# First layer of a fused two-block transformer kernel: decay's logarithm later, its square and the memory keys' scaling on ScalarE, recurrent parts in the MLP's buffer

## The reference, cut to what matters

```python
proj = h @ w_in;  u, gate, xq = split(proj, [512, 1024])
u = conv4(u) + conv_b                                  # depthwise, width 4
r = sigmoid(block_diag(u, w_r) + b_r); i = sigmoid(block_diag(u, w_i) + b_i)
log_a = -8.0 * r * softplus(-lam)                      # softplus needs a log1p
a = exp(log_a)
b = sqrt(-expm1(2.0 * log_a)) * (i * u)
hs = scan(h_t = a_t * h_{t-1} + b_t);  y = hs * gelu(gate)
k, v = split(rms_norm(mem) @ w_kv, 2)                  # memory keys and values
q, k = rms_norm(xq per head), rms_norm(k per head)     # 4 heads of 128
y_mem = softmax(q k^T / sqrt(128)) v
x = x + concat(y, y_mem) @ w_out
```

## Time and profile before

| | |
|---|---|
| median of 3 runs | 1368.66 us (1366.49 to 1369.4) |
| the profiled execution's own time | 1368.92 us |
| its span in the profile | 1366.8 us |
| TensorE busy | 1326.5 us, 97% of the span |
| VectorE busy | 869.9 us, 64% |
| ScalarE busy | 716.1 us, 52% |
| the chain that ended last | PE 83%, DVE 9%, ACT 3%, POOL 2% |
| mean granted TensorE clock | 0.988 of full speed |
| mean ScalarE copy of a unit, line 983 | 1048 ns |
| mean VectorE split of a unit, line 1538 | 1212 ns |

### The profile page before, as it was taken

How to read it: one execution, slowest core, us unless ns; L and a number is a source line. 1 busy time by engine, 2 the same in 40 slices (tenths; PEclk the granted TensorE clock), 3 DMA queues, 4 the chain that set the end, 5 groups by cost and what they waited for, 6 DMA issues and landing times.

```text
span 1366.8 us, 18745 instructions
## 1 busy us (share of the span) xinstructions
PE 1326.5 (97%) x7309; PEld 1132.7 (83%) x7309; DVE 869.9 (64%) x1154; ACT 716.1 (52%) x1177; POOL 122.1 (9%) x158
## 2 busy tenths in 40 slices
PE   6879999999999999999999999999999999999998
PEld 5868888887888888888988778888889887788887
DVE  4775656657645666567775666666676755666665
ACT  5565544546565545446554455555565444555553
POOL 2101100004201200003101020000021000100000
PEclk9999999999999999999999999999999998999999
DMA  9433655455423555545632145555356211555551
GB/s 363 165 123 122 232 186 197 172 186 201 170 80 121 200 199 186 186 172 192 206 111 76 48 170 186 193 187 196 136 199 218 93 63 62 172 190 189 189 186 46
DMA packets 62327, 224.43 MB, mean 164 GB/s; under 512 B 7192, under 2 KB 7328, under 8 KB 62240
## 3 DMA queue, kind: packets, MB, share of 16 engines
q1 hardware_dynamic: 59616, 214.23, 45.3%
q0 software_dynamic: 1904, 6.82, 1.5%
q10 hardware_dynamic: 720, 2.19, 0.4%
HBM read 222.16 MB, written 1.05 MB: 163 GB/s over the span
## 4 chain that ended last, share of the span: by engine, by line
PE 83%; DVE 9%; ACT 3%; POOL 2%; issue 2%; DMA 0%; ACTq 0%; POOLq 0%; DVEq 0%
PE ps L277 16%; PE ps L323 15%; PE ps L282 15%; PE ps L281 15%; PE ps L327 8%; PE ps L433 3%; PE ps L468 2%; DVE wlo L1538 2%; PE ps L330 2%; PE ps L491 2%; PE ps L797 2%; PE ps L329 1%; DVE xn L1577 1%; ACT xn L1020 1%; PE ps L472 1%
## 5 line engine op out<-in xcount | busy, mean ns | idle before, releaser
L1538 DVE TENSOR_TENSOR wlo<-raw,whi 128x1024 fp32r<-128x1024 f32 (+1 forms) x402 | 479.5, 1212 | 270.2 <-ACT whi L983 268.4
L983 ACT ACTIVATE whi<-raw 128x1024 fp32r<-128x1024 f32 (+1 forms) x409 | 424.1, 1048 | 289.7 <-PE ps L323 178.9
L323 PE MATMUL ps<-XT,whi 128*128 128x512 f32 x896 | 318.6, 399 | 0.0
L327 PE MATMUL ps<-XT,wlo 128*128 128x256 f32 x896 | 251.5, 281 | 0.0
L323 PEld LDWEIGHTS ps<-XT,whi 128*128 128x128 f32 x896 | 168.4, 188 | 41.1
L277 PE MATMUL ps<-whi,HT_hi 128*128 128x512 f32 (+1 forms) x496 | 187.5, 378 | 1.5 <-DVE wlo L1538 1.0
L282 PE MATMUL ps<-whi,HT_lo 128*128 128x512 f32 (+1 forms) x496 | 186.3, 376 | 0.0
L281 PE MATMUL ps<-wlo,HT_hi 128*128 128x512 f32 (+1 forms) x496 | 186.2, 375 | 0.0
L327 PEld LDWEIGHTS ps<-XT,wlo 128*128 128x128 f32 x896 | 169.3, 189 | 1.2
L277 PE MATMUL ps<-whi,XT 128*128 128x512 f32 (+1 forms) x304 | 122.5, 403 | 6.9 <-DVE wlo L1538 4.6
L282 PE MATMUL ps<-whi,XT 128*128 128x512 f32 (+1 forms) x304 | 118.0, 388 | 0.0
(11 more groups left out here) (254 smaller groups left out, 1845.1 us busy)
## 6 DMA issues: line engine op xcount, KB each, us to landing
raw<-in_w_m SPq DMA_DIRECT2D x152, 512.0 KB, 4.2
raw<-in_w_n SPq DMA_DIRECT2D x108, 512.0 KB, 4.2
raw<-in_w_c SPq DMA_DIRECT2D x48, 512.0 KB, 3.8
raw<-in_w_o SPq DMA_DIRECT2D x32, 512.0 KB, 3.5
raw<-in_w_kv SPq DMA_DIRECT2D x16, 512.0 KB, 4.5
raw<-in_w_b SPq DMA_DIRECT2D x16, 512.0 KB, 4.2
raw<-in_w_w SPq DMA_DIRECT2D x16, 512.0 KB, 5.5
raw<-in_w_a SPq DMA_DIRECT2D x12, 512.0 KB, 8.8
```

Source lines behind the costliest of these rows:

```text
L323: m = pe.matmul(outs[f][:, :], hi[:, j, at], both, start=(k == 0), stop=False)
L327: pe.matmul(outs[f][:, 0:T], lo[:, j, at], XT[0][:, k, :], start=False, stop=False)
L983: act.activation(whi[:, g % NSPLIT, 0:w], raw[:, g % NRAW, 0:w], ACT.Copy).then_inc(split_hi, 1)
L1538: dve.tensor_tensor(wlo[:, g % NSPLIT, 0:w], raw[:, g % NRAW, 0:w], whi[:, g % NSPLIT, 0:w].bitcast(F32), ALU.subtract).then_inc(split_lo, 1)
```

## The change

Five edits, all in layer 0:

1. On VectorE the `log1p` of the decay and the four small steps behind it stand after the convolution and not before the queries' sums. ScalarE waits for the biases (`hb`) ahead of the gates, and for the decay's constants (`lru_c`) only ahead of the decay.
2. (decay + 1)^2 is one Square on ScalarE; VectorE's two products become one.
3. The keys' scaling moves from two VectorE instructions of 128x512 to eight of 128x128 on ScalarE. Around it, one more unit's copy stands ahead of the square root, and VectorE splits unit 19 ahead of gelu.
4. The high and low parts of y go into `HT_hi` and `HT_lo`, `out_first` reads them there, and ScalarE's wait for the last product of `mv0` is gone.
5. In this attention's softmax VectorE makes the splits of units 20 to 22 one a step (`slowly`), where they stood together ahead of y's low part.

```diff
-            def out_first(L, w):
+            def out_first(L, w, rows=MX):
-                        linear(names, banks, [a[w][4 * nb + u]], 2, tok(MX), 2 * u, KT, opened=(u == 0))
+                        linear(names, banks, [a[w][4 * nb + u]], 2, tok(rows), 2 * u, KT, opened=(u == 0))
-            out_left = out_first(0, "w_o0")
+            out_left = out_first(0, "w_o0", tuple(h[:, 0] for h in HT))
...
-            act.wait_ge(ev("lru_c"), 1)
+            act.wait_ge(ev("hb"), 1)
             for g, dst in ((0, 1), (1, 2)):
...
             act.wait_ge(bank_free[fills["rg0.1"].bank], fills["rg0.1"].turn)
+            act.wait_ge(ev("lru_c"), 1)
             for dst, fn, c in ((11, ACT.Tanh, "lh"), (7, ACT.Exp, "lc")):
                 for f in range(4):
                     at = slice(f * T, (f + 1) * T)
-                    m = act.activation(slot(dst, 1024)[:, at], slot(1, 1024)[:, at], fn, bias=sm(c, 4)[:, f:f + 1],
-                                       scale=sm(c, 4)[:, f:f + 1])
-            m.then_inc(ev("decay"), 1)
+                    act.activation(slot(dst, 1024)[:, at], slot(1, 1024)[:, at], fn, bias=sm(c, 4)[:, f:f + 1],
+                                   scale=sm(c, 4)[:, f:f + 1]).then_inc(ev("decay"), 1)
+            act.wait_ge(ev("decay"), 8)
+            act.activation(slot(4, 1024), slot(7, 1024), ACT.Square, bias=1.0).then_inc(ev("decay2"), 1)
...
-            splits(fills["mk0.0"].pos)
+            splits(fills["mk0.0"].pos + 1)
             act.wait_ge(ev("b2"), 1)
...
             rows_in("mk0", hrow[:, :, :].rearrange("p a b -> p (a b)"), None)
+
+            act.wait_ge(ev("frstd"), 2)
+            for tt in range(TT):
+                ps = full(f"mk0.{tt}")
+                for h in range(4):
+                    m = act.activation(slot(5, 1024)[:, tt * BLK + h * P:tt * BLK + (h + 1) * P], ps[:, h * P:(h + 1) * P], ACT.Copy,
+                                       scale=sm("rk8", 8)[:, 4 * tt + h:4 * tt + h + 1])
+                free(f"mk0.{tt}", m)
...
             mem_keys_in(0)
-            splits(fills["mv0.1"].pos + AHEAD)
-            f = fills["mv0.1"]
-            act.wait_ge(bank_full[f.bank], f.turn)
             act.wait_ge(ev("yrow"), 1)
-            act.activation(MX[0][:, 0:4, :].rearrange("p f t -> p (f t)"), slot(4, 1024), ACT.Copy).then_inc(ev("yhi"), 1)
+            act.activation(HT[0][:, 0, :, :].rearrange("p f t -> p (f t)"), slot(4, 1024), ACT.Copy).then_inc(ev("yhi"), 1)
...
-            def soft(tags, between):
+            def soft(tags, between, slowly=False):
...
-                    ps = full(f"{tag}.s{i}", 0 if n else NSPLIT)
+                    ps = full(f"{tag}.s{i}", 0 if n or slowly else NSPLIT)
...
-                    splits(fills[f"{tag}.s{i}"].pos + AHEAD)
+                    f = fills[f"{tag}.s{i}"]
+                    splits(min(f.pos + AHEAD, f.need + n + 1) if slowly else f.pos + AHEAD)
...
-            dve.wait_ge(ev("lamexp"), 1)
-            log1p(l4, z, w4, t4)
...
-            step(dve.tensor_scalar(sm("lc", 4), l4, -4.0, None, ALU.mult))
-            step(dve.tensor_scalar(sm("lh", 4), l4, -2.0, None, ALU.mult))
-            dve.tensor_scalar(sm("hb", 8)[:, 0:8], cg("br", 0, 8), 0.5, None, ALU.mult).then_inc(ev("lru_c"), 1)
+            dve.tensor_scalar(sm("hb", 8)[:, 0:8], cg("br", 0, 8), 0.5, None, ALU.mult).then_inc(ev("hb"), 1)
             fox_sums(1, sm("cq", 16)[:, 0:8], hq(8, P).rearrange("p n d -> p (n d)"), P)
...
             dve.memset(sm("one", 1), 1.0).then_inc(ev("conv"), 1)
+            dve.wait_ge(ev("lamexp"), 1)
+            log1p(l4, z, w4, t4)
...
+            dve.tensor_scalar(sm("lh", 4), l4, -2.0, None, ALU.mult).then_inc(ev("lru_c"), 1)
...
-            dve.wait_ge(ev("decay"), 1)
-            step(dve.scalar_tensor_tensor(om, decay, 1.0, th, ALU.add, ALU.mult))
-            dve.scalar_tensor_tensor(s8, decay, 1.0, om, ALU.add, ALU.mult).then_inc(ev("b2"), 1)
+            dve.wait_ge(ev("decay2"), 1)
+            dve.tensor_tensor(s8, om, th, ALU.mult).then_inc(ev("b2"), 1)
...
             splits(fills["mk0.1"].pos + AHEAD)
-            for tt in range(TT):
-                ps = full(f"mk0.{tt}")
-                at = slice(tt * BLK, (tt + 1) * BLK)
-                m = scaled(slot(5, 1024)[:, at].rearrange("p (n d) -> p n d", d=P), ps[:, :], sm("rk8", 8)[:, 4 * tt:4 * tt + 4],
-                           2, P)
-                free(f"mk0.{tt}", m)
+            splits(fills["mv0.1"].pos)
...
             gelu()
-            splits(fills["mv0.1"].pos + AHEAD)
             rglru_lo()
-            soft(["ma0"], {1: second_gains, 3: lambda: rows_out(["ma0"], "ma0", 0, xn[:, 0, 512:1024])})
+            soft(["ma0"], {1: second_gains, 3: lambda: rows_out(["ma0"], "ma0", 0, xn[:, 0, 512:1024])}, True)
```

More of the change, by code:

```diff
@@ L1757, in _ @@
             gain_column(sm("mgcol", 2)[:, 0:1], P, rg("xaq0"), rg("xak0"))
-            dve.wait_ge(ev("lamexp"), 1)
-            log1p(l4, z, w4, t4)
-            step(dve.tensor_scalar(t4, lam, -1.0, 0.0, ALU.mult, ALU.max))
-            step(dve.tensor_tensor(l4, l4, t4, ALU.add))
-            step(dve.tensor_scalar(sm("lc", 4), l4, -4.0, None, ALU.mult))
-            step(dve.tensor_scalar(sm("lh", 4), l4, -2.0, None, ALU.mult))
-            dve.tensor_scalar(sm("hb", 8)[:, 0:8], cg("br", 0, 8), 0.5, None, ALU.mult).then_inc(ev("lru_c"), 1)
+            dve.tensor_scalar(sm("hb", 8)[:, 0:8], cg("br", 0, 8), 0.5, None, ALU.mult).then_inc(ev("hb"), 1)
             fox_sums(1, sm("cq", 16)[:, 0:8], hq(8, P).rearrange("p n d -> p (n d)"), P)
@@ L1787, in _ @@
             dve.memset(sm("one", 1), 1.0).then_inc(ev("conv"), 1)
+            dve.wait_ge(ev("lamexp"), 1)
+            log1p(l4, z, w4, t4)
+            step(dve.tensor_scalar(t4, lam, -1.0, 0.0, ALU.mult, ALU.max))
+            step(dve.tensor_tensor(l4, l4, t4, ALU.add))
+            step(dve.tensor_scalar(sm("lc", 4), l4, -4.0, None, ALU.mult))
+            dve.tensor_scalar(sm("lh", 4), l4, -2.0, None, ALU.mult).then_inc(ev("lru_c"), 1)
             splits(fills["gate.1"].pos)
@@ L1836, in rglru_lo @@
                 dve.wait_ge(ev("yhi"), 1)
-                dve.tensor_tensor(MX[1][:, 0:4, :].rearrange("p f t -> p (f t)"), om,
-                                  MX[0][:, 0:4, :].rearrange("p f t -> p (f t)").bitcast(F32), ALU.subtract).then_inc(ev("ylo"), 1)
+                dve.tensor_tensor(HT[1][:, 0, :, :].rearrange("p f t -> p (f t)"), om,
+                                  HT[0][:, 0, :, :].rearrange("p f t -> p (f t)").bitcast(F32), ALU.subtract).then_inc(ev("ylo"), 1)
             def second_gains():
```

## The result

The changed kernel takes 1364.24 us in the median of 7 runs (1363.56 to 1365.63), the kernel before 1367.68 in 7 runs beside it (1365.79 to 1369.4). The ratio is 0.9976 with a 95% interval of 0.9967 to 0.9985, so it is faster by 0.24%, 3.4 us, with 2.1 to 4.5 us possible. In a later set, with the same two kernels, the ratio was 0.9954 (0.9941 to 0.9966), 6.3 us. The forecast was 4.2 us and 1364.5. The profiled execution took 1363.56 us, its span is 1361.4 us (before 1366.8), its mean granted clock 0.991 (before 0.988).

The account below looks back on a forecast made before the run. TensorE is nearly always busy, so only its waits before about 103 us count. Terms reach 4.15, then 4.5 us at unit 20 after y and softmax; less 0.3 for clock, 4.2: 1364.5 us, range 1361.8 to 1368.0.

Parts of the forecast that it names:

- The logarithm: Ahead of unit 7's split: moving VectorE's constants frees 3.4 us plus 1.9 of half clock, less 0.2 for PSUM banks: 5.1.
- The square: ScalarE ahead of the root: the Square and one more unit copy eat 2.1 us, leaving a 3.0 gain at the root.
- The scaling: Keys' scaling ahead of the transposes: eight ScalarE passes take 2.18 us against VectorE's 1.29, a loss of 0.9.
- y's parts: Behind gelu: without the wait for the last values' product, y's high part starts at 88.7, the low part 5.7 us earlier.
- the freed buffer brings 5.7: Term of the sum at y's high and low parts: no wait for the last values' product, 5.7 us gained.
- one split a step: In the softmax: two splits of 1.16 us now stand ahead of step 2's maxima, taking off 2.3 us.
- The clock: Half clock from TensorE's idle pieces ahead of unit 16, around the transposes and in the softmax: 0.3 us set aside.
- nothing happens: Rival, 3%: the time ahead of unit 20 is retaken by another wait, such as ScalarE's for GpSimd: 1368.7 us.
- slower: Rival, 5%: half clock over the whole out projection; 14 us of it give 1371.5 us.
- The softmax does not hold it: Rival, 12%: step 2's maxima do not queue behind the two splits, so y's 5.7 us come through: 1362.9 us.
- The clock takes some back: Rival, 22%: one of units 20 to 24 at half clock, or the stretch at 43.20 staying; gain 1.7 to 2, 1366.8 us.

Follow-up runs that it names:

- root first: Changed kernel with scaling and Square back on VectorE, gelu's tanh and unit 16's copy behind ScalarE's square root: 1361.3 us, 0.9949 of the kernel before.
- best: As root first, plus queries' sum of squares behind unit 7's split and second layer's gain columns behind the last maxima: 1358.03 us, 0.9925 of the kernel before.

## Why the prediction was right

By its steps, in times from the reduction, predicted and measured in the changed kernel (the predicted ones are those of its text less 36.99):

| step | predicted | measured |
|---|---|---|
| unit 7's split | 1.5 | 1.5 |
| root | 32.9 | 32.9 |
| unit 16's first product | 37.1 | 37.3 |
| keys' sum | 40.4 | 40.4 |
| scaling starts, ends | 44.6, 46.8 | 44.6, 46.7 |
| unit 19's first product | 49.1 | 49.0 |
| y's high part | 51.7 | 51.6 |
| step 2's maxima | 59.8 | 59.5 |
| unit 20's first product | 62.4 | 62.3, 62.1 |

- *The logarithm*: right, and it carries the gain. Edit 1 alone takes 3.5 to 3.8 us off the path and measures 0.9968; the other four alone measure 0.9997. The 1.9 us of half clock went with the 3.4: the root moved by 5.1, which is 3.4 + 1.9 - 0.2. That the whole change has a path 0.8 to 1.3 shorter than edit 1 alone is no more than the half clock took from edit 1's two profiles (1.2 and 1.6), so that a gain of the other four on top is not shown.
- *The square*: right in sign and size. It costs 1.05 us at the root, and with the copy of unit 16 ahead of it 2.0, where the sum has 2.1.
- *The scaling*: 2.17 us on ScalarE as read from the eight passes at 8.55, against 1.29. What the text did not price is how much of the wait for GpSimd could have been filled: with the scaling undone, 1.9 us come back at unit 20, and the difference of the two durations is only 0.9. The other 1.0 is what is left for the copy held behind an in-order wait; with the copies ahead of that wait 1.3 to 1.5 came back. The Trainium skill, page "ScalarE: Activation LUTs", section "Rules for kernel authors", says to do multiplications on VectorE and not on ScalarE. The traces agree for the scaling, 1.29 against 2.17.
- *y's parts*: the times are right, the reason given in the sum is not. It says that "the freed buffer brings 5.7". Undoing the buffer alone costs 0.5 to 0.7 of path, at full clock in unit 19. y's high part came 6.0 us earlier because unit 19 and y did, and the buffer only spared a wait that would end half a microsecond after y. The terms of that sum were differences read at successive points and not values of edits, and only their total could be right. The same holds for the 2.3 us that the sum takes off for one split a step: undoing that edit costs 1.8 to 1.9.
- *The clock*: 0.3 were set aside, 0.16 came in the first profile. The half clock at unit 19 in the kernel before is missing from the working. It did no harm to the forecast, because y's high part, which waited for unit 19's products before, hangs on VectorE in the changed kernel; with edit 1 alone, where it still waits for them, it took up to 1.2 us.
- *From the path to the time*: the path won 4.6 to 4.8 us, the sets give 3.4 and 6.3. The rest is not in the path. In 14 profiles the stretch from unit 20 to the end takes 1260.7 to 1265.0 us, whichever kernel it is, and follows the time at half clock behind 110 us (added up from the granted clock of stretches of 1 us, to the last matmul): 1260.7 with 14 us of it, 1262.2 to 1262.7 with 17, 1263.0 to 1263.2 with 20, 1264.6 to 1264.7 with 24, 1265.0 with 27. The reduction itself starts at 34.7 to 37.2. Before's two profiles and after's two have tails of 1263.0, 1262.7, 1263.0 and 1260.7: nothing of the gain is given back later. That the median of 1364.24 lies 0.3 from the forecast is in part luck: the kernel before came out at 1367.68 beside it, 1.0 under the 1368.66 from which the forecast was taken off, and the later set gives 6.3 us and not 3.4.
- Of the rivals, "nothing happens" and "slower" did not occur. "The softmax does not hold it" did not either: step 2's maxima queued behind the two splits, and with the gain columns moved away as well the path got 1.0 us shorter (root first to best). "The clock takes some back" is what a single set of runs looks like when the tails differ, but not at unit 20.

Open: whether edit 1 alone reaches 61.8 without its longer half clock, and so what the other edits add to it; what each part is worth in time and not in path; whether the half clock at 43 us in the kernel before ever fails to come.

## What to carry to other kernels

Work that nobody needs yet, in front of the split that TensorE waits for, cost here its 3.4 us and 1.9 of half clock behind the gap; move it to where its user is 3 us away. On an engine that works in order, a wait is paid by all that is queued behind it: put ready work ahead of it, and count what stands ahead of a table load as part of the path. Moving passes to the less busy engine is no gain where that engine holds the path, as the Square and the scaling did here.

## What was not expected of the hardware

- The half clock is a large part of the scatter: the work behind unit 20, whose order is the same in the two kernels, takes 4.3 us more or less with 27 or 14 us of half clock in it, and executions of one kernel differ in that (the changed kernel's two by 20 against 14 us, and 2.3 us in the tail).
- The path itself repeats to 0.02 us between two executions of the kernel before, when the clock falls in the same places.
- Seven of the traces have a gap of 2.3 to 2.4 us ahead of unit 16. Half clock followed it in five, among them the second profile of the changed kernel, and not in the other two, its first profile (full clock until 93 us) and edits 2 to 5 alone. Nothing was lost by it in the changed kernel, since unit 19 hung on VectorE and ScalarE.
- A GpSimd instruction on 128x8 numbers took 2.50 us in the one profile in which VectorE was busy beside it and 1.65 in the 13 others.
